# The ring of split fp32 weights laid at 2064 bytes a tile in place of 2048

## The reference

```python
h = rms_norm(x, attn_norm_w[l])
proj = h @ w_in[l]                       # 2048 x 4624, split into q, k, v, z, xBC, dt
attn = sliding_window_attention(q, k, v, ...)   # 16 query heads, 4 kv heads, window 128, sinks
ssm  = mamba2_mixer(z, xbc, dt_raw, ...)        # causal conv, chunked scan, gated group norm
x = x + concatenate([attn, ssm]) @ w_out[l]     # 2048 x 2048
h = rms_norm(x, ffn_norm_w[l])
x = x + (silu(h @ w_gate[l]) * (h @ w_up[l])) @ w_down[l]   # 2048 x 5632, twice, and 5632 x 2048
```

## Time and profile before

| | |
|---|---|
| median of 2 runs | 2157.2 us (2157.01 to 2157.38) |
| the profiled execution | 2157.83 us, its span 2156.1 us |
| granted TensorE clock | 0.999 of full speed |
| PE busy | 2143.3 us, 99% of the span |
| PEld busy | 1941.3 us, 90% |
| DVE busy | 1198.6 us, 56% |
| ACT busy | 1001.7 us, 46% |
| DMA | 392.69 MB, mean 182 GB/s |

### The profile page before, as it was taken

How to read it: one execution, slowest core, us unless ns; L and a number is a source line. 1 busy time by engine, 2 the same in 40 slices (tenths; PEclk the granted TensorE clock), 3 DMA queues, 4 the chain that set the end, 5 groups by cost and what they waited for, 6 DMA issues and landing times.

```text
span 2156.1 us, 33054 instructions
## 1 busy us (share of the span) xinstructions
PE 2143.3 (99%) x14202; PEld 1941.3 (90%) x14202; DVE 1198.6 (56%) x1360; ACT 1001.7 (46%) x1250; POOL 112.7 (5%) x157
## 2 busy tenths in 40 slices
PE   9999999999999999999999999999999999999999
PEld 7888888999999999888888887899999999998887
DVE  5866665555555555544467666555555555554443
ACT  5555655444444444434445556544444444443332
POOL 2023110000000000000000222000000000000000
PEclk9999999999999999999999999999999999999999
DMA  7554356666666666565656544566666666666664
GB/s 219 176 166 131 122 173 177 201 192 193 194 195 196 193 193 193 189 196 190 190 164 184 156 123 127 182 186 194 191 194 195 195 195 192 192 194 204 204 197 137
DMA packets 202882, 392.69 MB, mean 182 GB/s; under 512 B 12224, under 2 KB 12592, under 8 KB 202736
## 3 DMA queue, kind: packets, MB, share of 16 engines
q1 hardware_dynamic: 201952, 388.67, 59.9%
q0 software_dynamic: 784, 1.90, 0.4%
HBM read 388.43 MB, written 2.10 MB: 181 GB/s over the span
## 4 chain that ended last, share of the span: by engine, by line
PE 98%; ACT 1%; issue 0%; POOL 0%; SPq 0%; DMA 0%; DVE 0%; DVEq 0%; ACTq 0%
PE ps L501 47%; PE ps L689 44%; PE ps L510 2%; PE ps L603 1%; PE ps L552 0%; PE ps L667 0%; PE ps L666 0%; PE ps L639 0%; PE ps L640 0%; PE ps L665 0%; POOL ys L468 0%; DMA vrows<-in_k_norm_w_dram 0%; PE ps L608 0%; PE ps L611 0%; PE ps L594 0%
## 5 line engine op out<-in xcount | busy, mean ns | idle before, releaser
L689 PE MATMUL ps<-h_hi,w_hi_s 128*128 128x256 f32 x2816 | 779.4, 277 | 0.0
L689 PE MATMUL ps<-h_hi,w_lo_s 128*128 128x256 f32 x2816 | 779.2, 277 | 0.0
L689 PE MATMUL ps<-h_lo,w_hi_s 128*128 128x256 f32 x2816 | 779.1, 277 | 0.0
L1079 DVE TENSOR_TENSOR w_lo<-raw,w_hi 128x1024 fp32r<-128x1024 f32 x384 | 476.0, 1243 | 381.7 <-ACT w_hi L839 380.5
L1079 DVE TENSOR_TENSOR w_lo_s<-raw,w_hi_s 128x1024 fp32r<-128x1024 f32 x352 | 431.1, 1225 | 437.1 <-ACT w_hi_s L839 437.1
L839 ACT CAST w_hi_s<-raw 128x1024 fp32r<-128x1024 f32 x352 | 369.5, 1050 | 527.5 <-PE ps L689 512.1
L839 ACT CAST w_hi<-raw 128x1024 fp32r<-128x1024 f32 x384 | 403.5, 1051 | 424.8 <-PE ps L501 406.7
L689 PEld LDWEIGHTS ps<-h_hi,w_hi_s 128*128 128x128 f32 x2816 | 529.3, 188 | 0.1
L689 PEld LDWEIGHTS ps<-h_lo,w_hi_s 128*128 128x128 f32 x2816 | 529.0, 188 | 0.1
L689 PEld LDWEIGHTS ps<-h_hi,w_lo_s 128*128 128x128 f32 x2816 | 528.8, 188 | 0.0
L501 PE MATMUL ps<-w_hi,f_hi 128*128 128x512 f32 x960 | 297.7, 391 | 0.0
(11 more groups left out here) (195 smaller groups left out, 1011.4 us busy)
## 6 DMA issues: line engine op xcount, KB each, us to landing
raw<-in_w_gate_dram SPq DMA_DIRECT2D x176, 512.0 KB, 3.7
raw<-in_w_up_dram SPq DMA_DIRECT2D x176, 512.0 KB, 3.6
raw<-in_w_down_dram SPq DMA_DIRECT2D x176, 512.0 KB, 4.7
raw<-in_w_in_dram SPq DMA_DIRECT2D x144, 512.0 KB, 3.6
raw<-in_w_out_dram SPq DMA_DIRECT2D x64, 512.0 KB, 4.7
out_dram<-xr SPq DMA_DIRECT2D x4, 512.0 KB, 6.4
xr<-in_x_dram POOLq DMA_DIRECT2D x3, 512.0 KB, 6.2
xr<-in_x_dram SPq DMA_DIRECT2D x1, 512.0 KB, 4.5
```

Source lines behind the costliest of these rows:

```text
L689: done = nc.tensor.matmul(ps[:, bank + m // 2, m % 2 * TOK:(m % 2 + 1) * TOK], w[:, slot, k, m * P:(m + 1) * P], h[:, rows + k, :], start= ...
L1079: v_.tensor_tensor(lo[:, slot, :, :], raw[:, slot, :, :], hi[:, slot, :, :].bitcast(F32), ALU.subtract).then_inc(lo_split, 1)
```

## The change

Each tile of the four names takes 516 columns of memory of which 512 are used, so that tiles are 2064 bytes apart. The gap between the rings shrinks so that the next buffer still starts at 67072 (two rings of 16512 bytes and gaps of 256 and 512 bytes). No buffer but these is moved.

```diff
         raw = sb("raw", [P, RING, 2, N], F32, 512)
-        w_hi = sb("w_hi", [P, RING, 2, N], F32R, 512)
-        sb("w_hi_gap", [P, P])
-        w_lo = sb("w_lo", [P, RING, 2, N], F32R, 512)
+
+        w_hi = sb("w_hi", [P, RING, 2, N + 4], F32R, 512)[:, :, :, 0:N]
+        sb("w_hi_gap", [P, P // 2])
+        w_lo = sb("w_lo", [P, RING, 2, N + 4], F32R, 128)[:, :, :, 0:N]
         sb("w_lo_gap", [P, P])
 
 
-        at_w, w_size = 33280, RING * 2 * N * 4 + P * 4
-        w_hi_s = nc.alloc_sbuf_tensor_at("w_hi_s", [P, RING, 2, N], F32R, offset=at_w + 64)
-        w_lo_s = nc.alloc_sbuf_tensor_at("w_lo_s", [P, RING, 2, N], F32R, offset=at_w + w_size + 64)
+        at_w, w_size = 33280, RING * 2 * (N + 4) * 4 + P * 2
+        w_hi_s = nc.alloc_sbuf_tensor_at("w_hi_s", [P, RING, 2, N + 4], F32R, offset=at_w + 64)[:, :, :, 0:N]
+        w_lo_s = nc.alloc_sbuf_tensor_at("w_lo_s", [P, RING, 2, N + 4], F32R, offset=at_w + w_size + 64)[:, :, :, 0:N]
```

## The result

The changed kernel takes 2215.45 us (2 runs, 2215.45 and 2215.46) against 2157.2: ratio 1.0268, 95% interval 1.0249 to 1.0287. It is slower by 58 us. The range held this, but the likeliest case did not come: the time is that of rival 1 with both forms, priced at 2213 us.

What follows compares the result with a forecast made beforehand. The prediction took the density of TensorE's matmuls as the bound: 2157.83 us for the profiled execution, + 1.4 for moving tiles, + 0 for the rest, = 2159.2, forecast 2159 us as the median; range 2150 to 2235 us.

Steps and rivals of the forecast that it cites:

- the likeliest case: Whole kernel: no visible effect, 2150 to 2170 us, chance 0.50.
- rival 1: TensorE's weight load and moving stream meet, slower cadence: part of the products 2170 to 2200 us, 0.14; both forms over 2200, 0.27.
- What bounds the kernel: TensorE is fed all the time, PE 99% busy; only how densely its matmuls follow each other can move the time.
- The splits at nothing: Splits at L839 and L1079, now walking two rows of 512: under 20 ns either way, hidden, costed at nothing.
- The moving tiles at 1.4 us: Moving weight tiles at L501, 4608 matmuls: 6 of 8 tiles touch one more 64-byte piece, 0.42 ns each, 1.4 us.
- the argument from proportion: Moving tiles: excess of 13.3 ns on 512 columns, 6.7 on 256, follows the columns, so no collision with the weight load.
- the sign that I had set: Reading of the 17th cycle is wrong if the moving form changes by more than 1 ns a matmul.
- The stationary tiles at nothing: Stationary weight tiles at L689, 8448 matmuls: only the weight load's home changes; taken as nothing.
- The row against the change: Start of gate products: same matmuls, tiles and homes at 117.9 and 117.8 ns, later 113.3; could be 36 us.
- the quiet case: Whole kernel: forecast of no visible effect, 2150 to 2170 us, chance 0.50.
- Rival 2: Matmul streams: the 17th cycle was due to the home; faster, 2112 us for moving tiles, 2041 for all; chance 0.07.
- Rival 3: A split becomes the bound and PE waits for it, 2249 us at worst; chance 0.02.

Runs made afterwards that it cites:

- run 6: The kernel before with all four weight buffers at home 64, activations at 0, tiles 2048 bytes apart: 2205.64 us beside 2159.03.
- run 5: The kernel before with all four weight buffers at home 0, activations at 0, tiles 2048 bytes apart: 2211.98 us beside 2159.03.
- runs 1 and 8: The kernel before with tiles 2112 bytes apart, 2218.68 us; the kernel before with all four weight buffers at home 192, activations at 0, 2184.73 us.
- run 12: The kernel before, all homes as there, with the two small transposes done after the third pair of the first up group, not the first: 2175.55 us beside 2159.21.
- run 11: The kernel before with only the activations h and f moved 16 bytes on, weights at their old homes 0 and 64: 2220.11 us beside 2159.21.
- run 9: The kernel before with all four weight buffers 256 bytes further on, tiles 2048 bytes apart: 2158.04 us beside 2159.21.
- run 4: The changed kernel with splits treating only 64 of 512 columns after the first four pairs of each way of multiplying: 2211.48 us, ratio 1.0248.

## Why the prediction was right in part and wrong in its likeliest case

- **What bounds the kernel** was read rightly: no wait of PE's weight loads grew by more than 0.2 us, the splits stayed at their ns, and the 58 us are the density of matmuls.
- **The splits at nothing**: right; 1243 and 1225 ns are unchanged to the ns. But "a better home gave 18 ns" was misread: with the homes exchanged the low split of the first way takes 1239 ns at home 64 (run 6) and that of the second 1224 at home 0 (run 5). The difference goes with the stage, not with the home.
- **The moving tiles at 1.4 us** failed. The term measured 17 us (57.6 less 40.3), 3.8 ns a matmul over all of them and 4.3 in the long runs. The step that failed is the argument from proportion. I took the excess of 1 in 16, which is in proportion to the columns, for the whole cost, as if nothing could be added to it; the runs show a second part that depends on the homes. That second part does not go with the columns: from the best to the worst long run it is 6.7 ns in the stationary form (113.3 to 120.0, 256 columns) and 6.6 in the moving one (226.7 to 233.3, 512 columns), some 16 cycles at 2.4 GHz in either. No long run of the fourteen kernels went under 113.3 or 226.7. Whether the first part is paid by 64 bytes, as I read it, no run shows, and by the sign that I had set, more than 1 ns a matmul, the reading does not stand as it was.
- **The stationary tiles at nothing** failed too: 40.3 us, 5.0 ns on the 8016 matmuls of the long runs. I leaned on 32 matmuls of the dt columns as proof that the home does not matter. They show 114.4 ns, but by the order of the buffers their homes are 64 and 192, so that 0, 80 and 128, which measured 120.0, 118.8 and 118.7 ns, are not among them. At their own homes, too, they took 118.4 ns in runs 1 and 8.
- **The row against the change** was the right one, and rival 1 built on it had place, sign and size: 2213 us for 2215.5. Its price of 4.5 ns a matmul was measured as 5.0, that of the moving form, 4.1, as 3.8. Part of this closeness is luck. The two errors have opposite signs, the 4.1 came from twelve products at homes 0 and 0 that include a start, and PE did not fall into the cadence of 117.8 but into an uneven one of 118.3. That the streams meet, as its name says, stays argued. I gave it 0.27 and the quiet case 0.50, though two cadences at one pair of homes were in the trace, and no row showed the moving form at a home other than 0. The Trainium skill's rule that loading the next weights takes nothing from the running matmul (TensorE: Matmul & The Clock Gate, Part 2, step 1) was no reason to price the term at nothing: by the weights' home alone the same stream runs at 113.3 (before) or 120.0 ns (run 5). Whether the load takes the time from the matmul, or something else does, no run shows.
- **Rival 2** did not come. The spacing that the Trainium skill gives for an isolated stream (the same page, Part 2, Back-to-back issue gap), 109.2 and 215.8 ns here, was reached at no home tried; the best are 113.3 and 226.7.
- **Rival 3** did not come: PE's weight loads waited for a split 0.7 us, as before.

## What to carry to other kernels

When TensorE hardly ever waits, divide the time of unbroken runs in the chain of waits by their matmuls and look whether one stream shows two values; if it does, SBUF placement is part of the schedule, and any move of a matmul operand by less than 256 bytes (a padding, a new buffer ahead of it) can cost up to 3%, as here. Choose the homes of both operands as a pair, keep every tile of a ring at it, and change one form of matmul at a time, since the pair that was good for one form here (64 against 0: 113.3 ns in the kernel before) is a bad one for the other (228.9 or 233.3). A good pair does not settle it: the same 64 against 0 ran at 117.8 in run 6, where only the home of other products had changed, so read the cadences anew after each change. An experiment that moves one operand only cannot tell a home from a difference; move both once.

## What was not expected of the hardware

- At one pair of homes the stream keeps one of two steady cadences: 113.3 or 117.8 ns for over 440 us (run 12), and 226.7 ns for 60 us or 233.3 for 246 us (run 11). As little as two transposes of 0.22 us changes it (run 12: 449.04 against 466.51 us for 3960 matmuls). So two kernels that differ in a harmless detail can be 17 us a layer apart.
- The weights moved by 256 bytes give the same cadences (run 9), and a common shift of both operands by 64 leaves the long runs at 454.26 and 239.40 us.
- ACT and DVE, writing and reading the same rings, make no difference to it in the changed kernel: 474.33 and 243.95 us with the full splits and with seven eighths of nearly every split left out (run 4).
